# One attention planner paced by counted score tiles in place of weighted widths, and six weight steps moved

## The reference, cut to what matters

```python
proj = rmsnorm(x) @ w_in           # q, k, v, z of both branches, forget logits, gates
# FoX: 8 heads of 64, per-frame causal, cumulative log-forget bias
s = q k^T / 8 + cq - ck ; p = softmax(s) ; of = p v
# differential: 4 heads, two maps each, relative bias near the diagonal, chunk mask
a = softmax(s0) - lam * softmax(s1) ; od = a v
out = x + (sigmoid(ga)*(yf @ w_up_f) + sigmoid(gb)*(yd @ w_up_d)) @ w_o
```

## Time and profile before

| What | Value |
|---|---|
| Median of three runs | 2804.83 us |
| Profiled execution: time, span | 2804.83 us, 2803.1 us |
| TensorE busy | 2697.1 us (96%) |
| VectorE, ScalarE busy | 1184.0 us, 1083.4 us |
| Prompt attention (pass B) | from 1425.3 us to 2395.5 us |

### The profile page before, as it was taken

The page is one execution under the profiler, slowest core; times in us unless marked ns, Lnnn a source line. Parts: engine busy times, 40 slices in busy tenths (PEclk is TensorE's granted clock), DMA queues, the critical chain, the costliest instruction groups (busy, mean ns, idle before and its releaser), DMA issues.

```text
span 2803.1 us, 37797 instructions
## 1 busy us (share of the span) xinstructions
PE 2697.1 (96%) x15257; PEld 2162.7 (77%) x15257; DVE 1184.0 (42%) x1847; ACT 1083.4 (39%) x2182; POOL 255.9 (9%) x270
## 2 busy tenths in 40 slices
PE   5999999999999999999989999999999999999998
PEld 4788888889999999999865665566566556888897
DVE  3421224315443332443333464365355446655554
ACT  3123331112122222100356676676666667422221
POOL 0100001131000000112230000000000003100000
PEclk9999999999999999999989999999999999999999
DMA  3453334448776766766651405053250503544442
GB/s 105 130 155 107 105 106 139 140 141 220 216 204 188 204 168 169 206 192 162 168 130 28 100 23 123 5 121 70 58 118 5 123 16 115 163 136 136 135 125 94
DMA packets 405774, 353.71 MB, mean 126 GB/s; under 512 B 45440, under 2 KB 368968, under 8 KB 399416
## 3 DMA queue, kind: packets, MB, share of 16 engines
q1 hardware_dynamic: 396464, 332.66, 44.1%
q0 software_dynamic: 9136, 18.63, 2.0%
HBM read 250.23 MB, written 100.71 MB: 125 GB/s over the span
## 4 chain that ended last, share of the span: by engine, by line
PE 86%; ACT 4%; DVE 3%; DMA 2%; issue 2%; POOL 1%; SPq 1%; DVEq 0%; ACTq 0%; POOLq 0%
PE p_acc L834 13%; PE p_acc L836 13%; PE p_acc L835 13%; PE a_sa L1887 5%; PE a_sa L1890 5%; PE a_sb L1907 4%; PE a_op L1936 4%; PE a_sb L1916 4%; PE a_op L1933 3%; PE p_turn L865 2%; PE e_U L1390 2%; PE e_U L1391 2%; PE e_U L1392 2%; ACT a_sa L1762 2%; ACT a_e L1791 2%
## 5 line engine op out<-in xcount | busy, mean ns | idle before, releaser
L834 PE MATMUL p_acc<-p_h_hi,p_w_hi 128*128 128x384 f32 (+1 forms) x1960 | 717.2, 366 | 9.8 <-DVE p_h_lo L652 5.8
L836 PE MATMUL p_acc<-p_h_hi,p_w_lo 128*128 128x384 f32 (+1 forms) x1960 | 702.0, 358 | 0.0
L835 PE MATMUL p_acc<-p_h_lo,p_w_hi 128*128 128x384 f32 (+1 forms) x1960 | 701.4, 358 | 0.0
L1813 DVE TENSOR_REDUCE a_nmax<-a_sa 128x1 f32<-128x1024 f32 (+7 forms) x384 | 349.4, 913 | 481.9 <-PE a_sa L1890 481.6
L1791 ACT ACTIVATE a_e<-a_sb 128x512 f32<-128x512 f32 (+3 forms) x640 | 317.9, 532 | 245.4 <-PE a_sb L1916 240.5
L834 PEld LDWEIGHTS p_acc<-p_h_hi,p_w_hi 128*128 128x128 f32 x1960 | 369.4, 188 | 45.2 <-issue 10.2
L836 PEld LDWEIGHTS p_acc<-p_h_hi,p_w_lo 128*128 128x128 f32 x1960 | 369.0, 188 | 31.5
L835 PEld LDWEIGHTS p_acc<-p_h_lo,p_w_hi 128*128 128x128 f32 x1960 | 369.8, 189 | 29.5
L1762 ACT ACTIVATE a_sa<-a_sa,a_nmax 128x1024 f32<-128x1024 f32 (+7 forms) x384 | 323.7, 843 | 73.3 <-DVE a_nmax L1813 71.9
L1887 PE MATMUL a_sa<-a_k,a_q 128*128 128x512 f32 (+4 forms) x640 | 261.6, 409 | 39.8 <-ACT a_sa L1762 33.3
L1907 PE MATMUL a_sb<-a_q,a_k 128*128 128x512 f32 (+2 forms) x640 | 272.5, 426 | 5.7 <-ACT a_e L1791 4.5
(11 more groups left out here) (217 smaller groups left out, 3490.4 us busy)
## 6 DMA issues: line engine op xcount, KB each, us to landing
p_raw<-in_w_in SPq DMA_DIRECT2D x98, 512.0 KB, 5.3
s_k_raw<-in_cache_fox_k SPq DMA_DIRECT2D x32, 512.0 KB, 6.9
s_v_raw<-in_cache_fox_v SPq DMA_DIRECT2D x32, 512.0 KB, 6.4
s_k_raw<-in_cache_diff_k SPq DMA_DIRECT2D x32, 512.0 KB, 7.1
s_v_raw<-in_cache_diff_v SPq DMA_DIRECT2D x32, 512.0 KB, 6.6
a_q<-scratch_q_hi SPq DMA_DIRECT2D x32, 512.0 KB, 13.8
a_k<-scratch_k_hi SPq DMA_DIRECT2D x32, 512.0 KB, 12.5
e_pair<-scratch_gT SPq DMA_DIRECT2D x80, 192.0 KB, 2.7
```

Source lines behind the costliest of these rows:

```text
L834: nc.tensor.matmul(acc[a % 2][:, 0:n], hi, h_hi[p][:, k, at:at + n], start=(k == 0), stop=False)
L835: nc.tensor.matmul(acc[a % 2][:, 0:n], hi, h_lo[p][:, k, at:at + n], start=False, stop=False)
L836: last = nc.tensor.matmul(acc[a % 2][:, 0:n], lo, h_hi[p][:, k, at:at + n], start=False, stop=(k == DK - 1))
L1813: nc.vector.tensor_reduce(nmax[:, b % 2, c, col:col + 1], scores_of(ev[1]), axes, ALU.max, negate=True).then_inc(a_maxed, 1)
```

## The change

Two edits. The planner's amount of pass A for each step of pass B was reckoned in weighted work (the unit's width plus STEP = 300, at a rate of 1.04 times the mean over all steps); it is now reckoned in units, at 1.25 units for each step. And in the last f, GpSimd's steps `W` 2 to 7 stand four merge slots later (12 to 17, before 8 to 13), and each load `LW` 8 + n two slots after `W` n (10 and 11 to 15 become 14 to 19), which puts `LW` 10 to 15 four slots later.

```diff
         for n in range(NH):
             slots[4 + n // 2] += [("LW", n)]
-            slots[6 + n] += [("W", n)]
-            slots[8 + n] += [("LW", NH + n)]
+            at = 6 + n if n < 2 else 10 + n
+            slots[at] += [("W", n)]
+            slots[at + 2] += [("LW", NH + n)]
...
     LEAD = 9
-    STEP = 300
-    a_work = list(itertools.accumulate([0] + [a_width(unit) + STEP for unit in A_UNITS]))
-    RATE = 1.04 * a_work[NA] / NU
+    RATE = 1.25
...
         def target(u):
-            need = max([a_work[a_last[x] + 1] - RATE * max(0, b_first[x] - LEAD - u) for x in range(2, NB)
+            return max([a_last[x] + 1 - RATE * max(0, b_first[x] - LEAD - u) for x in range(2, NB)
                         if b_first[x] - LEAD >= u] + [0])
-            return next(n for n in range(NA + 1) if a_work[n] >= need)
...
-            share = pass_a(target(u))
+            share = pass_a(min(NA, math.ceil(target(u))))
```

## The result

| | before | after |
|---|---|---|
| Median of six runs | 2808.39 us | 2834.05 us |
| Lowest and highest | 2801.11 to 2812.75 | 2825.84 to 2837.96 |
| Profiled execution: time, span | 2804.83, 2803.1 us | 2824.14, 2822.4 us |
| Mean granted clock, median over all recorded runs | 0.990 | 0.987 |

The changed kernel is slower: ratio 1.0088, interval 1.0074 to 1.0102. The forecast was 2798.6 us in a range of 2784 to 2817, with 0.12 for slower; the time is 17 us outside. The profiled execution of after is the fastest of its runs, with a clock of 0.989, so its trace shows a little less than the whole loss.

A forecast was written before the change was run, and what follows sets the result against it. TensorE, busy 96% of the span, was taken as the bound, with only its waits able to change. Opening -4.0, odd f -9.0, even f +4.7, f = 7 doubles +0.1, last constant +2.0: -6.2 from 2804.8 gives 2798.6 us, range 2784 to 2817.

The forecast's parts named there:

- Part 2: Odd f (differential): new doubles wait 2.8 us, old ones 5.3; taken as -3.0 us each, -9.0 for three f.
- the clock behind new holes: Granted clock could fall again in new waits of 1.4 us; a few us per fall, only widening the range.
- Part 1: Opening, pass B's first step: three units fewer save 6.9 us, their return in f = 7 costs 2.9; net -4.0 us.
- The rule itself: A step's second pass A unit can't start before 1.8 us plus the preceding unit's exponent, 1.2 us at width 1024.
- Part 3: Even f (FoX): all nine new doubles stand uncovered in even steps; +1.0 us each for f = 2, 4, 6, sum +4.7.
- Part 4: Last block: its constant comes one slot later, adding 2.0 us to pass B's wait of 1.26 us.
- Part 5: Last f: the moved weight steps `W` and `LW` change nothing in the time.
- The rival on the slower side: Wide doubles in even steps of FoX cost 1.4 us each and delay pass B's next exponent; 2822 us, chance 0.13.
- The rival that even pacing pays: In both kinds of f most of the loss in doubles goes; 2782 us at the far end, 2786 middle; chance 0.21.
- two signs of being wrong: Even and odd f move alike, or new time appears where pass B waits for its own exponents.

The follow-up runs named there:

- e7: After plus eight small identity products, results unused, in the hole of Q1's first step in every f; 2817.35 us, 1.0041 to before.
- e1: Before with only the moved `W` and `LW` slots, planner untouched; 2806.71 us, 1.0008 to before.
- e8: Before with pass A's units limited in the first steps of the attention, old order from then on; 2802.44 us, 0.9986 to before.
- e10: Before with one empty finishing stage moved ahead of the logarithm, which comes one stage later; 2807.12 us, 1.0004 to before.
- e2: After with the `W` and `LW` steps back in their old slots, so the new pacing alone; 2829.11 us, 1.0091 to before.
- e3: After with one empty finishing stage moved ahead of the logarithm, which comes one stage later; 2815.82 us, 1.0037 to before.
- e4: After with a quarter of a unit off the planner's need, so doubles stand one step later, in odd steps; 2795.63 us, 0.997 to before.
- e9: After with doubles in odd steps, the later logarithm and the last block's constants two steps earlier; 2787.44 us, 0.9933 to before.

## Why the prediction was wrong, by its own steps

**The steps that failed.** Two. Part 2's count of waits in the odd f had the old doubles at 5.3 us and the new at 2.8; the trace has TensorE idle for 2.6 and 3.8 us, and the f came out longer, not shorter. And the clock behind new holes was put at nothing in the sum; it made about a third of the loss, net of what the clock cost before. Both are worked out below.

**Where the 26 us are.** Time at a granted clock of 0.50 instead of 1.00 lowers the mean over the run by half its share. After's mean is 0.003 below before's: 0.003 x 2834 / 0.5 is 17 us at half clock more, in which half is lost, 8.5 us. e7 stands 0.0055 above after, which by the same working is 16 us, and it gained 13 to 17. It also stands above before, because the kernel before has half clock of its own which the new order lacks: its opening lasts longer, and the old order has falls in Q0 of an even f (f = 2 in before's trace, f = 4 in e1's, f = 4 and 6 in e8's, none in e10's). So the clock accounts for some 16 us gross, and for 8 to 9 net of what it cost before; the other 17 are waits. The means are rounded to 0.001, which makes each of these figures uncertain by 2 or 3 us. The profile of after has it in about the same proportion. It has six falls: five of some 1.6 us (Q1 of f = 0, 4, 5 and 6, and the end), and a longer one in f = 2 that costs 3.0 (129.0 us, against the 126.0 of e7's even f). That is some 11 us; less the 1.6 of f = 2 before, 9 of the +22.1. How many falls a timed run has was not seen, only its mean clock; e2's trace, the same planner, has eight.

**Part 1, the opening:** the term was right, the return was not. The first block is 8.3 us shorter (6.9 predicted), and the half clock lasts 20.5 us, before 27.3. But f = 0 as a whole gained 3.0, where 5.2 was forecast: its Q1 is 5.5 us longer (28.3, before 22.8) by the new hole and a fall behind it. e8 shows the opening by itself: -8.2 in the first step, 5.9 of it given back at once, 4 us in the median.

**Part 2, odd f:** -3.0 each predicted, +1.7 measured where no fall came with it. It is the largest term that had the wrong sign, 14 us in three f without falls. The old waits were reckoned at 5.3 us and were 2.6 in f = 5: Q1's and Q2's old doubles, put at 1.1 together, left TensorE no idle time, and the last two of Q3, put at 0.8 and 0.65, left 0.45 and about 0.1. The new ones were reckoned at 2.8 and were 3.8, of which 1.61 stand at Q1's first double (0.8 reckoned) and 1.15 in a step for which nothing was reckoned (below). The late logarithm is not the whole of it: in e3, without it, odd f still take 118.8 us, +1.0. The bound of "+1 (every wide double costs the 1.22 of the even f)" for one f was too low as well.

**The rule itself** failed in two places. It counts the exponents in ScalarE's line and nothing else; the list in Q1's first step also has the logarithm, and ahead of that a maximum on VectorE. Q1's first double was sized 1.35 in even f and 0.8 in odd; TensorE stood idle there for 2.24 and 1.61. With the logarithm moved behind the exponents (e3) it is 1.27 and 0.90. And it looks at the second unit of a step only. Q3's double with a 1024-wide and a 128-wide unit was put at 0.1 in even f and 0 in odd. It does cost nothing in its own step, but the next step's single unit comes up before the wide one's exponent is done. Timeline, after, f = 4, Q3 step 9, and that exponent:
```profile
2037.20 1.09 ACT L1760 ACTIVATE a_sa<-a_sa,a_nmax 128x1024 f32<-128x1024 f32 x1 [1.46 <-DVE a_nmax L1811]
2038.45 0.50 PE L1885 MATMUL a_sa<-a_k,a_q 128*128 128x512 f32 x1 [0.97 <-ACT a_sa L1760]
```
Of the nine waits that make f = 4's 7.7 us, three (0.97, 0.42 and 0.29) stand in steps that hold one unit.

**Part 3, even f:** right in direction and reason, +1.0 predicted, 126.0 - 123.9 = +2.1 measured in e7's f = 4, where no fall adds to it, and 125.3 - 123.9 = +1.4 in e3's f = 6, where the logarithm's part is gone too. That even f lose by the doubles' place is shown by e4: against those 126.0 it takes 121.4, 4.6 us less in each even f, with each double one step later. That it is the products standing between or ahead of the two units fits this, and that odd f, with one product in every step, gain only 0.7; no run varies it by itself.

**Part 4, the last constant:** right to 0.1 us, 1.94 us more wait for 2.0 predicted. GpSimd again loses 2.60 us before its fourth DMA; what it does there stays open. Not predicted was a clock fall behind the 3.20 us, some 1.6 us: the last block takes 34.5 us, before 32.9.

**Part 5, the weight steps:** right; e1 measures 1.0008, not told from 1. GpSimd's splits ran in one piece, soon after block 30's constants, as was said. (That they ran "without a gap of their own" before was misread: at 2322.05 they had waited 2.45 us for a load. Nothing hung on it.) First and last, after, answering to the earlier trace rows:
```profile
2333.07 0.64 POOL L1193 TENSOR_SCALAR e_up_hi<-e_x 128x512 fp32r<-128x512 f32 x1
...
2348.59 1.28 POOL L1199 TENSOR_TENSOR e_up_lo<-a_v,e_up_hi 128x512 fp32r<-128x512 f32 x1
```

**The rivals.** The second failed step is the last one there: "One further fall like it would cost a few us; this widens the range and is no case of its own." The price of one was right, 1.6 us here, but a pattern that repeats in eight f brings the fall back up to eight times, and then it is a case. Had it been priced as a rival, 1.6 us behind each of eight holes gives 13 us on top of the sum. The trace of the kernel before had a warning: its f = 2 takes 125.5 us, 1.6 more than f = 4 and 6, by a fall in its first block, behind waits that f = 4 has too without a fall. The prediction took one f of each kind to stand for all and did not name it. The rival on the slower side (2822 us, chance 0.13) was right that wide doubles in even steps pass 1.4 us, in one place of each f, and wrong about why: it has pass B's exponents late, and pass B's wait shrank. The rival that even pacing pays is refuted as the change has it; e4 and e9 show that even pacing does pay when the doubles stand where something covers them. The prediction gave two signs of being wrong; the first came true: even and odd f moved alike.

The Trainium skill ("TensorE: Matmul & The Clock Gate", "The HAM clock gate (the "warmup" mystery)") says that activity releases the throttle. The opening agrees, 6.8 us less of half clock after a chain that is 8.2 us shorter; so does e7, where more activity in a step of the same length kept the full clock.

## What to carry to other kernels

When a planner spreads work, ask for each doubled piece what stands between its two halves on the engine that waits; the count of doubles said nothing here, their place one step earlier or later was worth 4.6 us in 126. Ask it of the step behind as well. List everything that an in-order engine has in line at that moment, the small finishing operations and their own inputs included, since a 0.2 us logarithm cost 0.7 to 1.0 us in each f by waiting ahead of the exponents. And a new idle stretch that repeats needs two prices, its own and that of the clock behind it; filling it with idle products is a quick way to measure the second.

## What the runs showed of the hardware

A hole of 2.2 us in a step of 5.1, in a kernel whose TensorE is 96% busy, was followed by a step at a granted clock of 0.60, and holes of that length by a fall in 8 of 8 cases; behind 1.61 us a fall came in 4 of 8, behind e3's 1.27 us in 2 of 4 (f = 4 but not f = 6), behind 0.91 us in none of 4. Eight 128x128 products, 1.95 us of work, kept the clock at 1.00 and made the kernel 13 to 17 us faster, though they compute nothing. And a profiled execution can be the mild one: after's has a clock of 0.989, while its other runs have down to 0.984.
